# Latent attention stage of a four-layer kernel: values between two items' scores, and a new order of weight blocks, rope swaps, key sum and bank release

## The reference, cut to what matters

```python
def mla_mixer(h, w_dq, q_norm, w_uq, w_dkv, kv_norm, w_ukv, q_gain, k_gain, w_o):
    cq = rms_norm_2(h @ w_dq, q_norm)                      # 384 latent features for the queries
    q = (cq @ w_uq).reshape(b, s, MLA_HEADS, MLA_QK)       # 16 heads of 64 plain + 32 rope features
    dkv = h @ w_dkv
    ckv = rms_norm_2(dkv[..., :MLA_KV_RANK], kv_norm)      # 256 latent features for keys and values
    k_rope = broadcast(dkv[..., None, MLA_KV_RANK:])       # one rope part for all heads
    kv = (ckv @ w_ukv).reshape(b, s, MLA_HEADS, MLA_NOPE + MLA_V)
    k = concatenate([kv[..., :MLA_NOPE], k_rope]);  v = kv[..., MLA_NOPE:]
    q, k = rms_norm_2(q, q_gain), rms_norm_2(k, k_gain)    # per head
    q, k = plain parts with apply_rope(the rope parts, pos)
    o = chunk_causal_attention(q, k, v)                    # softmax in f32, mask by chunks of 64 tokens
    return o.reshape(b, s, MLA_HEADS * MLA_V) @ w_o
```

## Time and profile before

| | |
|---|---|
| median of three runs | 2576.47 us |
| profiled execution | 2577.62 us |
| its span, first to last instruction | 2575.8 us |
| TensorE busy | 2557.3 us (99%) |
| VectorE busy | 1662.4 us (65%) |
| ScalarE busy | 1276.7 us (50%) |
| GpSimd busy | 360.7 us (14%) |
| granted TensorE clock | full speed in all 40 slices |
| latent projections on TensorE | from 1480.6 to 1544.9 us |
| attention on TensorE | from 1542.3 to 1628 us, its first two steps inside the projections |

### The profile page before, as it was taken

The page is one execution under the profiler, slowest core; times in us unless marked ns, Lnnn a source line. Parts: engine busy times, 40 slices in busy tenths (PEclk is TensorE's granted clock), DMA queues, the critical chain, the costliest instruction groups (busy, mean ns, idle before and its releaser), DMA issues.

```text
span 2575.8 us, 35285 instructions
## 1 busy us (share of the span) xinstructions
PE 2557.3 (99%) x12630; PEld 2030.0 (79%) x12630; DVE 1662.4 (65%) x2398; ACT 1276.7 (50%) x2142; POOL 360.7 (14%) x270
## 2 busy tenths in 40 slices
PE   9999999999999999999999999999999999999999
PEld 7855788888777557888888775799988777899887
DVE  4476677643988895677653778597633546687533
ACT  4326543333546895444333578577533425567432
POOL 0020100000103782100000130000610002000800
PEclk9999999999999999999999999999999999999999
DMA  5330232223243442233222230232232221232222
GB/s 216 106 94 21 91 107 97 92 97 98 82 133 123 131 131 81 72 109 98 96 93 96 95 103 10 65 116 101 89 112 93 96 97 51 97 123 99 82 98 98
DMA packets 74833, 250.44 MB, mean 97 GB/s; under 512 B 8764, under 2 KB 9148, under 8 KB 74336
## 3 DMA queue, kind: packets, MB, share of 16 engines
q1 hardware_dynamic: 73632, 240.63, 28.5%
q0 software_dynamic: 944, 8.33, 0.9%
q10 hardware_dynamic: 144, 0.00, 0.0%
HBM read 242.50 MB, written 2.24 MB: 95 GB/s over the span
## 4 chain that ended last, share of the span: by engine, by line
PE 92%; DVE 3%; ACT 2%; issue 1%; DMA 1%; SPq 0%; POOL 0%; DVEq 0%; ACTq 0%; POOLq 0%
PE bank L432 25%; PE bank L433 24%; PE bank L434 24%; PE bank L1361 2%; PE bank L1363 2%; PE bank L1362 2%; PE bank L2257 2%; PE bank L2808 1%; PE bank L654 1%; PE bank L639 1%; PE bank L3156 1%; PE bank L1706 1%; PE bank L640 1%; PE bank L1695 1%; PE bank L2264 1%
## 5 line engine op out<-in xcount | busy, mean ns | idle before, releaser
L383 DVE TENSOR_TENSOR wlo<-wraw,whi 128x1024 fp32r<-128x1024 f32 x344 | 441.5, 1285 | 448.8 <-ACT whi L360 448.2
L360 ACT ACTIVATE whi<-wraw 128x1024 fp32r<-128x1024 f32 x348 | 366.9, 1056 | 508.5 <-DMA wraw<-in_w 508.3
L432 PE MATMUL bank<-hnhi,whi 128*128 128x512 f32 (+1 forms) x1528 | 596.7, 390 | 1.1 <-DVE wlo L383 0.7
L433 PE MATMUL bank<-hnlo,whi 128*128 128x512 f32 (+1 forms) x1528 | 584.5, 383 | 0.0
L434 PE MATMUL bank<-hnhi,wlo 128*128 128x512 f32 x1392 | 542.1, 389 | 0.0
L432 PE MATMUL bank<-ahi,whi 128*128 128x512 f32 x1184 | 463.5, 391 | 1.9 <-DVE alo L712 1.1
L434 PE MATMUL bank<-ahi,wlo 128*128 128x512 f32 x1184 | 460.8, 389 | 0.0
L433 PE MATMUL bank<-alo,whi 128*128 128x512 f32 x1184 | 460.8, 389 | 0.0
L432 PEld LDWEIGHTS bank<-hnhi,whi 128*128 128x128 f32 x1528 | 287.2, 188 | 86.3 <-issue 29.5
L433 PEld LDWEIGHTS bank<-hnlo,whi 128*128 128x128 f32 x1528 | 287.4, 188 | 57.5 <-issue 3.4
L434 PEld LDWEIGHTS bank<-hnhi,wlo 128*128 128x128 f32 x1392 | 261.3, 188 | 55.7
(11 more groups left out here) (360 smaller groups left out, 3940.5 us busy)
## 6 DMA issues: line engine op xcount, KB each, us to landing
wraw<-in_w SPq DMA_DIRECT2D x410, 512.0 KB, 3.3
arena<-cs_scratch SPq DMA_DIRECT2D x20, 512.0 KB, 5.9
over_a<-cs_scratch SPq DMA_DIRECT2D x12, 512.0 KB, 6.1
arena<-in_rpb POOLq DMA_DIRECT2D x1, 2880.0 KB, 14.1
arena<-in_t_step POOLq DMA_DIRECT2D x2, 897.0 KB, 5.1
mT<-arena SPq DMA_DIRECT2D x28, 64.0 KB, 2.0
out_dram<-xT SPq DMA_DIRECT2D x7, 256.0 KB, 2.0
arena<-in_t_ab POOLq DMA_DIRECT2D x1, 1472.0 KB, 6.7
```

Of the source, the lines that this page charges most:

```text
L360: act.activation(whi[:, slot * BLOCK:(slot + 1) * BLOCK], wraw[:, slot * BLOCK:(slot + 1) * BLOCK], ACT.Copy).then_inc(sem("w_hi"), 1)
L383: dve.tensor_tensor(low_home(i), wraw[:, slot * BLOCK:(slot + 1) * BLOCK], whi[:, slot * BLOCK:(slot + 1) * BLOCK], ALU.subtract).then_inc ...
L432: pe.matmul(out, wh, ah, start=start, stop=False)
L433: pe.matmul(out, wh, al, start=False, stop=False)
```

## The change

SyncE issues weight block 4 of the stage before swap 0, and then one block and one swap in turn; GpSimd issues the key's swap at the head of its part, on a semaphore of its own. VectorE turns the key at slot 3 instead of 2 and the four queries at slots 5, 8, 11 and 14 instead of 2, 5, 8 and 11. In the last slot of the projections TensorE puts step 1 ahead of the last key sum; ScalarE takes that key's root after its slot 4 of the attention, and VectorE writes the key after its step 2. The banks of the first transposes change. From step 4 to step 15 the values of item 2s-5 stand between the plain scores of the step's two items. The first two rows of the output projection wait for the maximum of item 31, the next for that of item 32.

```diff
                     sp.wait_ge(sem("dt_rows"), 3)
                     for h in range(5):
                         ssd_load(sp, h)
-                if lo == query + 4:
-                    sp_mla_rotary(sp, 0)
-                    sp_mla_rotary(sp, 1)
                 for i in tiles(sp, lo, hi) if lo not in (Z0 + 5, query + 4) else map(At, range(lo, hi)):
                     sp.wait_ge(sem("w_used"), i.value(1, -3))
                     sp_load(sp, i)
-                    if lo == query + 4 and i.base - lo in (1, 2, 4):
-                        sp_mla_rotary(sp, {1: 2, 2: 3, 4: 4}[i.base - lo])
+                    if lo == query + 4 and i.base - lo < 4:
+                        mla_rotary_moves(sp, (0, 2, 3, 4)[i.base - lo])
                     if lo == Z0 + 5:
                         sp_rows(sp, i.base - lo)
             for f in range(2):
...
 
         def mla_moved(i):
 
-            return sem(f"moved{i % 2}"), (288, 272)[i % 2] + 128 * (i // 2 + 1)
-
-        def sp_mla_rotary(sp, i):
-
             if i == 1:
-                sp.wait_ge(sem("krope"), 2)
+                return sem("moved_key"), 128
+            return sem(f"moved{i % 2}"), (288, 272)[i % 2] + 128 * (i // 2 + 1 - i % 2)
+
+        def mla_rotary_moves(eng, i):
+
+            if i == 1:
+                eng.wait_ge(sem("krope"), 2)
             else:
-                sp.wait_ge(sem("rope_read"), 3 * (i - (i > 0)) + 1)
+                eng.wait_ge(sem("rope_read"), 3 * (i - (i > 0)) + 1)
             if i == 3:
-                sp.wait_ge(sem("krope"), 4)
+                eng.wait_ge(sem("krope"), 4)
             elif i >= 2:
-                sp.wait_ge(sem("q_built"), i // 2)
+                eng.wait_ge(sem("q_built"), i // 2)
             src = krope() if i == 1 else q_rope(i - (i > 0))
             half = MLA_ROPE // 2
             for lo in range(0, P, half):
                 a = lo + half if lo // half % 2 == 0 else lo - half
-                sp.dma_start(mla_sin(i)[lo:lo + half, :], src[a:a + half, :]).then_inc(mla_moved(i)[0], 16)
+                eng.dma_start(mla_sin(i)[lo:lo + half, :], src[a:a + half, :]).then_inc(mla_moved(i)[0], 16)
 
         def sp_rows(sp, j):
 
...
             return arena[:, a:a + 1024]
 
         def mla_turn_banks(n):
-            return (7, 6) if n % 2 == 0 else (6, 7)
+            return (7, 6) if n in (0, 1, 3) or n >= 4 and n % 2 == 0 else (6, 7)
 
         def krope_sq():
             return over_a[:, 0:SEQ]
...
         MLA_EARLY = {26: 0, 28: 1}
 
         MLA_SPLITS = [0, 2, 4, 6, 8, 10, 12, 16, 22]
+
+        MLA_ROPES = [5, 8, 11, 14]
 
         def mla_split(i):
             return At(FIRST["mla_q"] + MLA_SPLITS.index(i) + 2)
...
                     project(i)
                 if i == 2:
                     pe_latent_sums(pe, 1)
+                if i in MLA_EARLY and MLA_EARLY[i] == 1:
+                    pe_mla_step(pe, 1)
                 if i >= 2:
                     kind, j = UNITS[i - 2]
                     if kind == "q":
                         query_sums(j)
                     if kind == "k":
                         key_sums(j)
-                if i in MLA_EARLY:
-                    pe_mla_step(pe, MLA_EARLY[i])
+                if i in MLA_EARLY and MLA_EARLY[i] == 0:
+                    pe_mla_step(pe, 0)
 
         def act_mla_proj(act):
             def square_pair(s, src):
...
                     act_rsqrt(act, bank[1][:, 0:64], q_scale, 1.0, MLA_QK * EPS, "q_scaled")
                     act.wait_ge(sem("q_scaled"), 1)
                     act.activation(q_minus, q_scale, ACT.Copy, scale=-1.0).then_inc(sem("q_scaled"), 1)
-                if i == len(UNITS):
-                    key_root(7)
                 if i >= 2 and UNITS[i - 2] in [("k", j) for j in range(7)]:
                     key_root(UNITS[i - 2][1])
+            act_mla_soft(act, (4, 5))
+            key_root(7)
 
         def pool_mla(pool):
 
+            mla_rotary_moves(pool, 1)
             for s in range(16):
                 pool.wait_ge(sem("pair_read"), s + 1)
                 if s < 8:
...
                     dve_split(dve, mla_split(i))
                 if i == 4:
                     dve_latent_norm(dve, 1)
-                if 2 <= i < len(UNITS) and UNITS[i - 2][0] == "rope":
-                    rope(UNITS[i - 2][1])
-                if i == 2:
+                if i == 3:
                     dve_rope_key(dve, 1)
+                if i in MLA_ROPES:
+                    rope(MLA_ROPES.index(i))
                 if i == 7:
                     dve_latent_low(dve, 1)
                 if i == 12:
...
                 if 2 <= i < 28 and UNITS[i - 2][0] == "k":
                     j = UNITS[i - 2][1]
                     dve_key(dve, j, ("plain", "rope") if j < 6 else ("plain",))
-            dve_mla_soft(dve, (1, 2))
+            dve_mla_soft(dve, (1, 3))
             dve_key(dve, 7, ("plain",))
 
         def mla_block(n):
...
                 for x in range(2):
                     if s:
                         pe.wait_ge(sem("item_max"), n0 + 2 * s - 1 + x)
+                    if x == 1 and s >= 4:
+                        values(2 * s - 5)
                     for e in range(2):
                         lo, hi = rows(e)
                         pe.matmul(bank[2 * x + e][:, 0:w], q_plain(2 * g + x, lo, hi)[:, c:c + P],
...
                 if n == 0:
                     pe.wait_ge(sem("proj_read"), 8)
                 if n == 1:
+                    pe.wait_ge(sem("item_turned"), n0 + 1)
+                if n == 2:
                     pe.wait_ge(sem("head_rsqrt"), 8)
                 both = n and max(w, MLA_ITEMS[n - 1]["w"]) > SEQ // 2
                 if n >= 2 or both:
...
                 pe_row(pe, "mla_o", j, lo, hi)
             if 2 <= s <= 17:
                 turn(2 * s - 3)
-            if s >= 3:
+            if s == 3 or s >= 16:
                 values(2 * s - 5)
             if s == 17:
                 pe_row(pe, "mla_o", 1, 0, 2)
...
 
         def act_mla(act):
             act_mla_proj(act)
-            act_mla_soft(act, (4, 38))
+            act_mla_soft(act, (5, 38))
 
         def dve_mla(dve):
             dve_mla_proj(dve)
-            dve_mla_soft(dve, (2, 17))
+            dve_mla_soft(dve, (3, 17))
 
         def mla_ready(eng, k):
             eng.wait_ge(sem("mla_out"), k.value(1, 1))
...
         def mla_banks(pe, m):
             n0 = len(NA_ITEMS)
             if m == 0:
+                pe.wait_ge(sem("item_max"), n0 + 31)
+            if m == 2:
                 pe.wait_ge(sem("item_max"), n0 + 32)
             if m == 4:
                 pe.wait_ge(sem("mla_out"), 7)
...
```

## The result

The changed kernel takes 2587.39 us (median of 6 runs, 2585.89 to 2589.54), the kernel before 2576.61 beside it (2576.43 to 2577.13): a ratio of 1.0041, 95% interval 1.0031 to 1.0051, 10.8 us slower. The forecast was 2580.4 (+3.9) with a range up to 2584.5: right in sign, outside the range, at a third of the size. The profiled execution is the longest of the six, 2589.54 (span 2587.8, 12.0 above before).

A forecast was written before the change was run, and what follows sets the result against it. The prediction took TensorE, busy 99% of the span, as the bound. Projections +3.9 us and attention 0 (start, middle and end together) on a median of 2576.47 gave 2580.4 us, with 8 in 10 for 2574.5 to 2584.5.

The forecast's parts named there:

- the projections' chain: Projections: late rotations hold swaps and the weight blocks queued behind them, delaying TensorE by 3.9 us.
- TensorE stalls there some 2.6 us: Projections, at the value 0 unit: TensorE waits some 2.6 us for a late weight block to be split.
- u15: Projection unit value 1: waits for ScalarE's read of the value 0 unit, starts at 1524, 3.9 us late.
- rival C: Key's swap on GpSimd: issues at 1.0 us or more, first query sum stalls 1.5, 2582; chance 0.15.
- L8: Weight block in SyncE's queue, behind the swap waiting for the second rotation: issued at 1519.4, before at 1507.5.
- L4's early issue: First weight block in SyncE's new queue: issued ten microseconds earlier, gives back 1.0 us of late query sums.
- Rival B: Loads do not hurt, L8 issued by about 1516: -1.0 in projections, -2 in attention, 2573.5; chance 0.20.
- In the other pan are the stalls inside the scores: Attention, steps 4 to 15: stalls of 3.05 us in all, set against +4.3 for the extra blocks.
- The sign of being wrong: Attention: forecast is wrong if the stretch from step 5 to step 15 differs by over 2 us.
- Rival D: Attention: blocks cost as forecast, stalls return as waits for a maximum or copy, +2.5 more, 2583; chance 0.15.
- Key sum: Last key sum behind step 1's scores fills the wait before step 2's scores: -0.8 us by step 4's end.
- banks: Output projection's first row waits for item 31's maximum instead of item 32's: -0.6 us.

The follow-up runs named there:

- experiment 2: Kernel before with the attention's part of the change alone (values between scores, key sum, banks): 2579.38 us, ratio 1.0015.
- experiment 1: Kernel before with the projections' part of the change alone (queue order, key's swap on GpSimd, later rotations): 2583.31 us, ratio 1.0028.
- Experiment 5: experiment 1 plus eight dummy matmuls into an unused bank where TensorE otherwise stands: 2581.37 us, ratio 1.0022.
- experiment 6: experiment 1 with VectorE's query rotations back at slots 2, 5, 8 and 11: 2575.46 us, ratio 0.9998.
- experiment 8: Whole change without values between scores, and with each weight load ahead of a waiting swap: 2573.91 us, ratio 0.9992.
- experiment 4: experiment 2 without values between the two items' scores, so key sum and banks only: 2574.19 us, ratio 0.9994.
- experiment 3: experiment 2 with the values put ahead of the wait for the maximum in TensorE's list: 2579.02 us, ratio 1.0013.
- experiment 9: experiment 3 with ScalarE's copy of the odd output bank ahead of that slot's exponentials: 2578.42 us, ratio 1.0010.
- experiment 10: experiment 8 plus values between scores in steps 4, 7, 11 and 15 alone, ahead of the maximum's wait, and the early copy: 2574.31 us, ratio 0.9994.
- experiment 11: experiment 8 repeated unchanged in more rounds: 2573.93 us, ratio 0.9992.

## Why the prediction was wrong

Two terms failed. The attention was put at 0 and lost 3.8 us by itself (experiment 2); the projections were put at +3.9 and lost 7.7 (experiment 1). The sign came out right by the projections' chain alone.

**Projections, forecast +3.9, measured +7.7. The failed step is "TensorE stalls there some 2.6 us".** The stall was costed as time that passes, and the matmuls behind it at their old pace. In fact TensorE stood for 1.39 and 2.53 us, its granted clock fell to 0.50, and u13, the query sums, u14 and a key sum ran at half pace. So u15's start was set by TensorE again, at 1527.63, and not by ScalarE's read of u13, which ended at 1525.3. Experiment 5 takes away nothing but the standing still and gets back 2.9 us of this stretch in the two traces (2.1 by the medians). The page that bears on it is the Trainium skill, "TensorE: Matmul & The Clock Gate", section "Wait — 56ns, not 53.3ns?": matmuls of 512 columns follow each other at 427 ns at the lower clock; this trace has 425 (four distances, 1520.31 to 1522.01), against 230 before. The forecast left the lower clock out.

The rest of that chain held in its order, not in all its sizes. GpSimd's swap was hidden, and quicker than forecast: 0.48 us an issue against 0.71, so rival C is out. L6 went out at 1506.9 (forecast 1506.1) and L8 at 1520.0 (1519.4). L7 was 2.0 late: the first rotation ended 0.7 later (the latent norm took 2.43 and not 1.9), R3 began 0.4 later behind L6 and took 5.88 us and not 5.05. Without the clock the loss is 5.3 by the trace of experiment 5 and 5.6 by the medians, against 3.9, a mis-sized term. Of the 1.4 between 3.9 and 5.3, u15 itself is 0.5 late. Another 0.4 was taken off for a key sum running into u15, though from u15's start to step 0 it takes 22.2 in experiment 5 as before. And 0.6 is the trace of before, which was slower here than five others. For the same reason L4's early issue gave back 0.65 by the traces of experiments 6 and 8 and 0.3 to 0.5 by the medians, and not 1.0: part of the delay that it was to cure was not there in the other executions. Rival B was the right question ("it decides on L8: issued by about 1516"): experiments 6 and 8, with L8 at 1512.8 and 1512.7, have no such loss, and experiment 8 comes within 0.4 us of rival B's 2573.5.

**Values between scores, forecast +4.3 for blocks less about 3 for stalls, so about +1.4, measured +5.2 by experiments 2 and 4. The failed step is "In the other pan are the stalls inside the scores", summed there to 3.05.** The price was right (0.35 a step by experiment 4). The gain was not there, for two reasons. First, I had read the code's order wrongly: the wait for the maximum stands ahead of the values, so they fill no stall (0.65 us in step 11 of the trace after, where it was 0.54). Second, experiments 3, 9 and 10 show that the right order would have given little, 0.4 us and 0.6 more of the 5.2: the long stalls coincide with the copy of the output bank, and when that is moved too, most of the time comes back as a wait for ScalarE's copies.

In the attention TensorE's listed waits came to 3.8 us in experiment 2 against 2.2 in experiment 4: longer with the values between, not shorter. Twelve times 0.35 is 4.2, and with these 1.6 it is 5.8. In steps 4, 11 and 15 the scores were parted by a wait already, so the 0.21 for cutting them falls away three times: 5.2, an estimate that meets the measured 5.2. The sign of being wrong that the prediction names, a stretch from step 5 to step 15 over 2 us off, came: it is 5 us longer. Rival D said that stalls "come back as waits for the first item's maximum or for a copy", at +2.5; it named this mechanism, and I gave it 0.15.

**Key sum, forecast -0.8; banks, forecast -0.6: right.** Step 0 to step 4 got 0.9 shorter; the distance from the last transposes of step 15 to the output projection went from 1.67 to 1.01 (experiment 4, and experiment 11 above), 0.66. In the trace before:

```profile
1619.17 1.06 PE L2829 MATMUL bank<-base_t,arena 128*128 128x128 f32 x8 [0.17 <-ACT arena L2876]
1620.84 0.47 PE L432 MATMUL bank<-ahi,whi 128*128 128x512 f32 x1 [0.61 <-DVE stats L2917]
```

Together experiment 4 gives -1.4 by the medians, as forecast.

**The sum.** With the sizes by the medians: 5.6 for the chain, 2.1 for the clock, -1.4 for key sum and banks, +5.2 for the values: 11.5, against 10.8 measured. The two parts hardly act on each other (7.7 + 3.8 = 11.5); the 0.7 that is missing lies within the spread of the six executions (2585.89 to 2589.54).

**Left open.** Whether a shorter stall would cost the clock as well was not tried. Nor does any run say why the low stretch was shorter in some executions than in others. Whether key sum and banks would each be seen alone was not tried either; their sizes are from traces.

## What to carry to other kernels

Before moving DMAs in a queue, write down for each load which waiting transfer stands ahead of it: a load that waits for nothing goes ahead of a swap that waits for an engine. Cost a stall of TensorE with what may run behind it at the lower clock, and hold against it that a few idle-time matmuls can be cheaper than standing. A stall may be filled only if the work put there was not itself covering the next wait; check first that the fill stands ahead of the wait in the list, and what its own output bank waits for. And read the size of a stall from more than one execution before you count on getting it back.

## What the runs showed of the hardware

- TensorE stood 1.39 and 2.53 us with eight small matmuls in between; during the second of these its granted clock fell, to 0.50 for about 10 us (in experiment 1 it stood 1.39 and 2.02 us, with the same outcome). Eight dummy matmuls of 256 columns in the same gaps kept it at 1.00.
- GpSimd issued eight DMAs of 32 KB in 3.87 us, 0.48 each; SyncE took 4.93 to 5.88 for such a set in the trace after, 0.62 to 0.74.
- A further block costs TensorE 0.14 us for values (64-column tiles) and 0.21 for scores (64-row tiles). In the traces of experiments 2 and 4 this does not depend on its length: values blocks of 4, 8, 12, 16, 20 and 28 matmuls take 0.37, 0.59, 0.80, 1.02, 1.25 and 1.68 us, one item's scores of 128, 256, 384 and 512 columns 0.43, 0.63, 0.85 and 1.06. The Trainium skill, "TensorEngine Tiling (Array Packing)", section "Key Properties", says that a change of tiling mode drains the engine. The blocks here change mode at each border, which fits, but no run separates the drain from other causes.
